# Top-k rounds ahead of the mixers' steps on VectorE, in the feed-forward stages of a two-layer trunk

## The chip, the cores and the metric

One core of a Trainium2 chip runs the whole kernel. The metric is the device time of one execution in microseconds (us). TensorE's clock has two levels, 1.2 and 2.4 GHz; the profile gives the granted clock as a share of full speed.

## The reference, cut to what matters

Two layers over a sequence of 1024 tokens, width 1024, float32. Each layer has three mixers side by side and then a feed-forward network:

```python
for l in range(DEPTH):                       # DEPTH = 2
    proj = rmsnorm(x, norm_mix[l]) @ w_in[l]
    y_a = s5_mixer(u, ...)                   # state space model, 16 groups
    y_b = dsa_attention(dq, dk, dv, iq, ik, iw, rel_bias)
    y_c = retention(rq, rk, rv, rg, ret_gn[l])
    x = x + concat(y_a, y_b, y_c) @ w_out[l]
    gate, up = split(rmsnorm(x, norm_ffn[l]) @ w_ffn_in[l], 2)
    x = x + (silu(gate) * up) @ w_ffn_out[l]     # D_FF = 2816
return rmsnorm(x, norm_final)
```

In `dsa_attention` an indexer scores every earlier position for each query, `lax.top_k` keeps 256 of them, and eight heads attend to these alone. The queries go in 8 blocks of 128; block b can see 128(b+1) keys, so blocks 0 and 1 need no choice.

## The kernel before, in words

The tokens are worked in two halves of 512. For layer l and half h there are three products: `proj` (18 units), `mixout` (8) and `ffn` (75). A **unit** is one 128-column slice of a weight matrix against all 512 tokens. Each number is split in a high and a low part, so a unit of `proj`, `mixout`, `gate` or `up` is 24 matmuls of 512 columns; a `down` unit is 12 (first of the four chunks of D_FF) or 18. Units write two psum banks in turn (A, B): unit i can begin only when unit i-2 has been read out. TensorE is the engine that should never stand.

Reading a unit out is VectorE's first work when the next unit has begun (the plan calls `ffn(..., i, ...)`, which handles unit i-1): the product of a gate with the row's scale (L1308), after which ScalarE applies Silu and GpSimd scales again; `up` times that (L1319); or the addition to x for a `down` unit (L1179). ScalarE also makes the high part of each weight tile (L835) and GpSimd the low part (L724).

All other work is cut into **steps** that stand in the plan behind a unit. Every engine walks the same list `PLAN` in order and issues its own part of each entry, so the order in the list is the order within each engine's queue. Three kinds matter here:

- `("round", b, r)`: one round of the top-k of block b, on VectorE alone (`top_round`): MAX8 finds eight largest scores of each row (L1359), MATCH_REPLACE8 strikes them out (L1361). Block b takes up to 32 rounds. Behind the last one a compare turns the scores into a mask (L1366 or L1368), which GpSimd needs for the attention of that block.
- `("attend", l, h, b, j, s)`: attention of block b for head pair j. In s=0 TensorE multiplies the probabilities of the pair before with the values and then makes the new logits (banks C and D). In s=1 VectorE adds mask and bias to the logits and takes the row's minimum of the negative (L1395, `nmax`, once for each head), ScalarE takes the exponential with that as bias (L1054), and TensorE transposes the result (L2079). These three stand in one step: TensorE reaches the transposes when the unit's matmuls are issued, and then needs VectorE's and ScalarE's part of the same step. With j=0, s=0 VectorE also makes the row sums of the block before (L1373, L1374), in s=1 it scales that block's output (L1381).
- `("scores", ...)` and `("retention", ...)`: the indexer's scores of a block (L1345 to L1352) and the pieces of the retention mixer (L1422 to L1483). In several of them too TensorE waits, at the end of the unit, for VectorE's part of the same step.

`weave(main, side)` (L84) deals the steps of a list over the units by estimated cost. It sorts what falls behind one unit; the sort is stable. The sides with both kinds are long in three stages: `ffn` of (0,0) and of (1,0), which carry the mixers of half 1 with the rounds of blocks 4 to 7, and `ffn` of (0,1), which carries those of layer 1, half 0, with the rounds of block 3. Other stages place their steps by hand or have no unit with both kinds behind it in another order.

In the stages of (0,0) and (1,0) the 96 rounds of blocks 5, 6 and 7 lie beside the attention of blocks 4, 5 and 6, which is 12 head pairs (four for each block). These stretches run from about 560 to 840 us and from 1851 to 2131 us; `ffn` of (0,1) with its mixers runs from 1111 to 1499 us.

Of the kernel before, what the change touches and what calls it, by code (L numbers as in the profile page):

```python
# [68 lines left out]
def cost(step):  # L69

    if step[0] == "round":
        return 2.2 * (NK[step[1]] + 150) / 1000
    return {"dma": 1.0, "diag": 1.0, "s5_prep": 3.0, "scores": 7.0}.get(step[0], 5.0)


def length(unit):

    kind, i = unit[0], unit[3]
    if kind == "ffn" and i < len(FFN) and FFN[i][0] == "down":
        return 3 * FF_CHUNKS[FFN[i][1]]  # L80
    return 3 * KT


def weave(main, side, first=0, last=None, rounds_last=True):  # L84


    last = len(main) if last is None else last
    total = sum(cost(s) for s in side) or 1.0
    time = sum(length(u) for u in main[first:last])
    out, n, spent, gone = [], 0, 0.0, 0  # L90
    for i, unit in enumerate(main):
        out.append(unit)
        gone += length(unit) if first <= i < last else 0
        share, behind = total * gone / time, []
        while n < len(side) and spent + cost(side[n]) / 2 <= share:
            spent += cost(side[n])
            behind.append(side[n])
            n += 1
        out += sorted(behind, key=lambda step: step[0] == "round") if rounds_last else behind
    return out + side[n:]  # L100


# [47 lines left out]
def plan():  # L150
# [16 lines left out]
    main = window("proj", 0, 0)  # L167
    side = [("boot", t) for t in range(TT + 1, NB + 2)] + [("bias", s) for s in range(3)]
    out += weave(main[:4], blend(param_steps(0), side)) + main[4:5] + [("rstd", "boot"), ("diag",)]
    sc = score_steps(0, 0)  # L170
    setup = [("s5_set", 0, s) for s in range(5)]
# [34 lines left out]
    def mix_and_ffn(l, h, side, lead):  # L206

        mix = window("mixout", l, h)
        ffn = window("ffn", l, h)
        got = []  # L210
        for n, unit in enumerate(mix[:N_OUT]):
            got += [unit] + (lead[n] if n < len(lead) else [])
        got += [("fillraw", DEPTH + l, 0)] + mix[N_OUT:] + [("fillraw", DEPTH + l, 1), ("sums", "inside")]
        got += ffn[:1] + scales() + weave(ffn[1:], side, 0, len(ffn) - 11)
        if (l, h) == (0, 0):

            for n, step in enumerate(param_steps(1)[:10]):
                got.insert(got.index(ffn[45 + 2 * n]), step)
        return got
# [4 lines left out]
    out += main[:1] + [("sums", None)]  # L224
    side = [("rstd", None), ("diag",), ("spread", "fill")] + [("dma", "load_xa", n) for n in range(4)] + param_steps(1)[10:14]
    out += weave(main[1:N_OUT], side)
    drain = main[N_OUT:]
    main = window("proj", 1, 0)
# [2022 lines left out]
```

## Time and profile before

| what | us |
|---|---|
| runs shown (3): median, lowest to highest | 2672.77, 2666.86 to 2673.14 |
| profiled execution: its own time | 2670.3 |
| its span, first to last instruction | 2668.5 |
| TensorE matmuls busy | 2551.4 (96%) |
| VectorE busy | 1553.0 (58%) |
| ScalarE busy | 1020.3 (38%) |
| GpSimd busy | 1308.9 (49%) |

Busy shares are means over stages: a slice of the 40 in the page's second part is 66.7 us, and there an engine at 58% over the span may be full for long stretches. A row of the timeline gives start, duration, engine, line, operation, output and inputs, and in brackets how long the engine stood before it and for whom. A matmul's duration (0.39 us for 512 columns) overlaps the next one's: from start to start it is 0.23 us.

### The profile page before, as it was taken

The page shows a single profiled execution, that of the slowest core. Times are in us where ns is not written, and L with a number is a line of the kernel's source. Part 1 is how long each engine was busy: PE and PEld are TensorE (multiplying, and loading weights), DVE is VectorE, ACT ScalarE, POOL GpSimd, SP SyncE. Part 2 cuts the span into 40 slices and gives each one's busy share as a digit, 9 for nine tenths or more (in the row PEclk, how much of TensorE's full clock was granted, in tenths as well). Part 3 has the DMA queues.
Part 4 walks back from the last instruction along what each step waited for, and adds up shares of the span by engine and source line. Part 5 has one row for each costly group of instructions (what it writes and reads, how often), then busy time and mean ns, then how long its engine had stood idle before and what let it go on. Part 6 is the DMA issues. An engine that isn't in the chain of part 4 may idle for free.

```text
span 2668.5 us, 34623 instructions
## 1 busy us (share of the span) xinstructions
PE 2551.4 (96%) x13515; PEld 2007.8 (75%) x13515; DVE 1553.0 (58%) x2691; ACT 1020.3 (38%) x1478; POOL 1308.9 (49%) x818
## 2 busy tenths in 40 slices
PE   8998979999999999999999999999999999999998
PEld 6766757677777777778777787777777777888887
DVE  3769767799997226833331385677999922211111
ACT  5232354244435433324344422442534453322222
POOL 3332344455545564536555532544555447665654
PEclk9988999999999999999999999999999999999998
DMA  5341112132222153323322242222222215233332
GB/s 165 85 132 41 49 53 90 52 91 72 78 71 64 58 189 95 87 64 91 91 77 82 80 138 56 79 60 76 77 77 60 79 44 201 79 103 103 108 110 82
DMA packets 385666, 232.91 MB, mean 87 GB/s; under 512 B 29593, under 2 KB 371553, under 8 KB 383073
## 3 DMA queue, kind: packets, MB, share of 16 engines
q1 hardware_dynamic: 385136, 229.62, 29.0%
q8 instruction: 109, 1.79, 0.3%
q10 hardware_dynamic: 368, 1.08, 0.1%
q14 instruction: 53, 0.43, 0.0%
HBM read 213.88 MB, written 14.69 MB: 86 GB/s over the span
## 4 chain that ended last, share of the span: by engine, by line
PE 68%; DVE 25%; ACT 3%; issue 3%; POOL 1%; DMA 1%; DVEq 0%; ACTq 0%; SPq 0%
PE psum L1759 65%; DVE scores L1361 7%; DVE top L1359 7%; PE psum L2079 1%; DVE psum L1395 1%; DVE xs L1179 1%; DVE scores L1347 1%; DVE tmp L1319 1%; ACT w_hi L835 0%; ACT scratch L1036 0%; POOL w_lo L724 0%; DVE tmp L1308 0%; DVE scratch L1428 0%; PE psum L2176 0%; ACT xs L1054 0%
## 5 line engine op out<-in xcount | busy, mean ns | idle before, releaser
L724 POOL TENSOR_TENSOR w_lo<-w_raw,w_hi 128x1024 fp32r<-128x1024 f32 (+2 forms) x408 | 900.8, 2208 | 1197.9 <-ACT w_hi L835 1197.8
L1759 PE MATMUL psum<-h_hi,w_hi 128*128 128x512 f32 x1984 | 796.4, 401 | 15.2 <-ACT h_hi L859 7.4
L835 ACT ACTIVATE w_hi<-w_raw 128x1024 fp32r<-128x1024 f32 (+2 forms) x408 | 397.7, 975 | 1047.9 <-PE psum L1759 989.4
L1759 PE MATMUL psum<-h_lo,w_hi 128*128 128x512 f32 x1984 | 763.2, 391 | 0.9 <-POOL h_lo L732 0.9
L1759 PE MATMUL psum<-h_hi,w_lo 128*128 128x512 f32 x1984 | 514.4, 390 | 0.0
L1759 PEld LDWEIGHTS psum<-h_hi,w_hi 128*128 128x128 f32 x1984 | 374.9, 189 | 128.3 <-issue 36.1
L1759 PEld LDWEIGHTS psum<-h_lo,w_hi 128*128 128x128 f32 x1984 | 373.9, 189 | 78.3 <-issue 1.9
L1759 PEld LDWEIGHTS psum<-h_hi,w_lo 128*128 128x128 f32 x1984 | 373.3, 188 | 76.6
L1359 DVE MAX8 top<-scores 128x8 f32<-128x512 f32 (+5 forms) x352 | 324.3, 921 | 7.8
L1361 DVE MATCH_REPLACE8 scores<-top,scores 128x512 f32<-128x512 f32 (+5 forms) x352 | 319.0, 906 | 0.0
L1179 DVE TENSOR_TENSOR xs<-xs,psum 128x512 f32<-128x512 f32 x160 | 109.6, 686 | 315.0 <-PE psum L1759 304.5
L1759 PE MATMUL psum<-a_hi,w_hi 128*128 128x512 f32 x704 | 279.2, 397 | 7.2 <-POOL a_lo L806 7.2
L1759 PE MATMUL psum<-a_lo,w_hi 128*128 128x512 f32 x704 | 274.9, 390 | 0.0
L1319 DVE TENSOR_TENSOR tmp<-psum,tmp 128x512 f32<-128x512 f32 x88 | 60.8, 691 | 245.0 <-PE psum L1759 243.9
L1759 PE MATMUL psum<-a_hi,w_lo 128*128 128x512 f32 x704 | 182.7, 393 | 0.0
L1759 PEld LDWEIGHTS psum<-a_hi,w_hi 128*128 128x128 f32 x704 | 132.6, 188 | 41.9 <-POOL a_lo L806 8.9
L1759 PEld LDWEIGHTS psum<-a_hi,w_lo 128*128 128x128 f32 x704 | 133.5, 190 | 28.1
L1759 PEld LDWEIGHTS psum<-a_lo,w_hi 128*128 128x128 f32 x704 | 132.7, 188 | 26.5
L806 POOL TENSOR_TENSOR a_lo<-tmp,a_hi 128x512 fp32r<-128x512 f32 x88 | 116.9, 1329 | 30.8 <-ACT a_hi L942 30.8
L1308 DVE TENSOR_TENSOR tmp<-psum,tmp 128x512 f32<-128x512 f32 x66 | 45.6, 691 | 122.1 <-PE psum L1759 114.8
L1759 PE MATMUL psum<-w_hi,h_hi 128*128 128x512 f32 x256 | 102.8, 402 | 4.4 <-ACT iqT L905 4.3
L1759 PE MATMUL psum<-w_hi,h_lo 128*128 128x512 f32 x256 | 100.5, 393 | 0.0
(310 smaller groups left out, 2913.5 us busy)
## 6 DMA issues: line engine op xcount, KB each, us to landing
w_raw<-in_w_ffn_in_dram SPq DMA_DIRECT2D x176, 512.0 KB, 3.8
w_raw<-in_w_ffn_out_dram SPq DMA_DIRECT2D x96, 384.0 KB, 3.1
w_raw<-in_w_in_dram SPq DMA_DIRECT2D x68, 512.0 KB, 3.8
w_raw<-in_w_out_dram SPq DMA_DIRECT2D x32, 512.0 KB, 3.6
x_half<-xs SPq DMA_DIRECT2D x8, 1024.0 KB, 6.5
xs<-x_half SPq DMA_DIRECT2D x8, 1024.0 KB, 6.9
w_raw<-in_w_ffn_out_dram SPq DMA_DIRECT2D x32, 256.0 KB, 2.7
out_dram<-mixed SPq DMA_DIRECT2D x8, 512.0 KB, 4.5
```

What stands on the lines that cost most here:

```text
L724: eng.tensor_tensor(w_lo(u, n), w_raw[:, u % 3, 0:n], w_hi[:, u % 2, 0:n].bitcast(F32), ALU.subtract).then_inc(sems["weights_ready"], 1)
L806: eng.tensor_tensor(a_lo[:, f, :], atmp, a_hi[:, f, :].bitcast(F32), ALU.subtract).then_inc(sems["a_lo_ready"], 1)
L835: act(w_hi[:, u % 2, 0:n], w_raw[:, u % 3, 0:n], ACTF.Copy).then_inc(sems["hi_ready"], 1)
L1179: tt(xs[:, m, :], xs[:, m, :], bank(g), ADD).then_inc(sems["x_added"], 1)
L1308: tt(scaled, bank(g), row, MUL).then_inc(sems["gated"], 1)
L1319: tt(atmp, bank(g), gate, MUL).then_inc(sems["atmp_ready"], 1)
L1347: ins = stt(score[b], bank(g, 0, NK[b]), w, score[b], MUL, ADD)
L1359: eng.max(out=top8[:, :], in_=src).then_inc(sems["round_step"], 1)
L1361: eng.match_replace(out=src, in_to_replace=top8[:, :], in_values=src, imm_value=TAKEN).then_inc(sems["round_step"], 1)
L1395: eng.tensor_tensor_reduce(bank(g, 0, nk), bank(g, 0, nk), at_.mask(b, n), -1.0, 3e38, ADD, ALU.min, nmax[:, i:i + 1]).then_inc(sems["nmax ...
L1759: return eng.matmul(out_, lhsT, rhs, start=start, stop=stop, skip_group_check=True)
L2079: ins = eng.transpose(bank(g, k * P, (k + 1) * P), at_.prob[:, n, k * P:(k + 1) * P], ident)
```

## The change

```diff
-def weave(main, side, first=0, last=None, rounds_last=True):
+def weave(main, side, first=0, last=None, sort_rounds=True):
...
-        out += sorted(behind, key=lambda step: step[0] == "round") if rounds_last else behind
+        out += sorted(behind, key=lambda step: step[0] != "round") if sort_rounds else behind
```

Before, the steps behind a unit stood with the mixers' steps first and the rounds last. Now the rounds stand first and the mixers' steps behind them. No step moves to another unit, and none is added or dropped; the order among rounds, and among the others, stays. No call passes the last parameter. The order changes behind 85 units: 36 of `ffn` (0,0), 36 of `ffn` (1,0) and 13 of `ffn` (0,1). Rounds issue on VectorE alone, so only VectorE's queue has another order; the queues of TensorE, ScalarE, GpSimd and SyncE stand as before, the DMAs too.

## Rows read from the trace of the kernel before

**Rows 1.** The page's slices: busy tenths of TensorE and VectorE over the span.
```profile
PE   8998979999999999999999999999999999999998
DVE  3769767799997226833331385677999922211111
```

**Rows 2.** The page's chain of work that ended last, by line.
```profile
PE psum L1759 65%; DVE scores L1361 7%; DVE top L1359 7%; PE psum L2079 1%; DVE psum L1395 1%; DVE xs L1179 1%; DVE scores L1347 1%; DVE tmp L1319 1%; ACT w_hi L835 0%; ACT scratch L1036 0%; POOL w_lo L724 0%; DVE tmp L1308 0%; DVE scratch L1428 0%; PE psum L2176 0%; ACT xs L1054 0%
```

**Rows 3.** Windows: PE, PEld, DVE, ACT, POOL busy us, PEclk, DMA share, GB/s.
```profile
560.00:840.00 280.00, 269.88 (x1453) 214.26 (x1453) 269.81 (x393) 122.39 (x163) 148.28 (x100) 0.99 0.26 75
1111.00:1499.00 388.00, 385.46 (x1927) 304.05 (x1925) 135.14 (x254) 155.73 (x247) 198.81 (x134) 1.00 0.28 81
```

**Rows 4.** Groups of VectorE by form, 560 to 850 us: busy us, mean ns.
```profile
L1359 DVE MAX8 top<-scores 128x8 f32<-128x1024 f32 x32 | 39.2, 1224 | 0.6
...
L1359 DVE MAX8 top<-scores 128x8 f32<-128x896 f32 x32 | 34.9, 1091 | 0.7
...
L1359 DVE MAX8 top<-scores 128x8 f32<-128x768 f32 x32 | 30.7, 958 | 0.7
L1361 DVE MATCH_REPLACE8 scores<-top,scores 128x768 f32<-128x768 f32 x32 | 30.2, 943 | 0.0
```

**Rows 5.** Timeline of the unit that began at 575.80, attention (4, pair 0).
```profile
575.80 0.39 PE L1759 MATMUL psum<-h_hi,w_hi 128*128 128x512 f32 x1
...
577.84 0.69 DVE L1308 TENSOR_TENSOR tmp<-psum,tmp 128x512 f32<-128x512 f32 x1
...
578.44 0.82 DVE L1395 CUSTOM_DVE_ANT_0 psum<-psum,scores 128x640 f32<-128x640 f32 x1
...
579.21 1.28 ACT L1054 ACT_TABLE_LOAD   x1
...
579.42 1.98 PE L1759 MATMUL psum<-h_hi,w_lo 128*128 128x512 f32 x8
...
580.50 0.80 ACT L1054 ACTIVATE scratch<-psum,nmax 128x640 f32<-128x640 f32 x1
...
581.53 1.51 PE L2079 MATMUL psum<-cst,scratch 128*128 128x128 f32 x10
...
582.80 0.47 PE L1759 MATMUL psum<-h_hi,w_hi 128*128 128x512 f32 x1
```

**Rows 6.** Timeline of the unit that began at 681.15, attention (5, pair 1).
```profile
681.15 0.39 PE L1759 MATMUL psum<-h_hi,w_hi 128*128 128x512 f32 x1
...
683.87 0.96 DVE L1395 CUSTOM_DVE_ANT_0 psum<-psum,scores 128x768 f32<-128x768 f32 x1
...
684.92 0.90 ACT L1054 ACTIVATE scratch<-psum,nmax 128x768 f32<-128x768 f32 x1 [0.30 <-DVE nmax L1395]
...
686.60 1.47 PE L2079 MATMUL psum<-cst,scratch 128*128 128x128 f32 x12
```

**Rows 7.** Timeline, attention (6, pair 1): late read-out, Silu, late values.
```profile
764.64 0.69 DVE L1308 TENSOR_TENSOR tmp<-psum,tmp 128x512 f32<-128x512 f32 x1
...
767.71 1.75 PE L1759 MATMUL psum<-scratch,vw 128*64 128x128 f32 x28 [2.51 <-ACT scratch L1036]
```

**Rows 8.** TensorE's waits before transposes, timeline; and one window as in rows 3.
```profile
807.52 2.84 PE L2079 MATMUL psum<-cst,scratch 128*128 128x128 f32 x14 [2.27 <-ACT scratch L1054]
...
892.42 3.12 PE L2079 MATMUL psum<-cst,scratch 128*128 128x128 f32 x16 [2.71 <-ACT scratch L1054]
...
807.90:811.40 3.50, 3.50 (x16) 3.17 (x15) 3.43 (x4) 1.47 (x3) 2.84 (x3) 0.51 0.25 48
```

**Rows 9.** Timeline of scores and retention, four waits between 459 and 551 us.
```profile
459.03 2.34 DVE L1347 SCALAR_TENSOR_TENSOR scores<-psum,vw,scores 128x896 f32<-128x896 f32 x2 [2.94 <-ACT psum L1029]
...
485.38 1.97 PE L2106 MATMUL psum<-cst,scratch 128*128 128x128 f32 x16 [1.50 <-DVE scratch L1428]
...
544.85 1.22 DVE L1469 TENSOR_REDUCE gsum<-scratch 128x16 f32<-128x1024 f32 x1 [1.67 <-ACT scratch L1082]
...
550.18 0.47 PE L1759 MATMUL psum<-h_hi,w_hi 128*128 128x512 f32 x1 [1.41 <-DVE xs L1179]
```

## The prediction

> **What bounds the kernel now.** I read the page's slices first: TensorE stands at 9 tenths nearly everywhere, VectorE at 7 to 9 in two places, slices 9 to 13 and again 28 to 32 [rows 1]. The chain says the same: 65% of it is TensorE's unit matmuls, but 14% is rounds (L1359 and L1361) and 1% is L1395 [rows 2]. So in those two places VectorE's queue sets the end. The windows size it: from 560 to 840 us TensorE is busy 269.9 of 280 and VectorE 269.8 of 280; in the third stage that the change touches VectorE is busy 135 of 388 and TensorE 385 [rows 3]. The first two are balanced to a hair: neither engine has slack, so what counts is who waits for whom, and a new wait of TensorE on VectorE costs nearly its length. The third has slack on VectorE. Last I read the timeline unit by unit, noting when TensorE began a unit, when VectorE read out the one before, and what ended TensorE's wait at its end.
>
> **What an attention step looks like.** The unit that begins at 575.80 has its last matmuls until 581.40. VectorE comes 2.0 late, reads out at 577.84 and goes straight to nmax at 578.44; ScalarE's exponential follows at 580.50 and the transposes begin at 581.53, just as the matmuls end. The next unit starts at 582.80 [rows 5]. The rounds of that unit run beside the transposes and the next unit. nmax is thus the one piece of VectorE's work with a near deadline, and it stands first. The step of (5, pair 1) is alike: nmax 683.87, exponential 684.92, transposes 686.60, which the matmuls and not the exponential delayed [rows 6].
>
> **The change, priced.** Nothing is added or removed; VectorE's busy time stays. The rounds of a unit now stand ahead of nmax. A round is MAX8 and MATCH_REPLACE8 and about 0.14 us between: 0.958 + 0.943 gives 2.05 us for block 5, and from MAX8's 1.091 and 1.224, with a replace of like length, 2.3 us for block 6 and 2.55 us for block 7 [rows 4].
>
> The way from the start of nmax to the first transpose is 1.05 us to the exponential, 0.90 of it and 0.2 for its sum: 2.15 us at 768 columns [rows 6], so about 1.85 at 640 and 2.4 at 896. The table load at 579.21 began before the first nmax had ended [rows 5]; with rounds in between it is hidden, so it isn't in these sums.
>
> First place, (4, pair 0): nmax would start 2.65 us into the unit; with two rounds (4.1) it is 6.75, and the transposes come at 8.6 where the matmuls end at 5.6. TensorE stands 3.0. The next unit starts at 9.9 where it was 7.0: +2.9. Is it given back? VectorE leaves nmax early against the next unit (about 1 us before it starts, its read-out done), runs that unit's two rounds in 4.1 and then must wait for the unit to end at 5.7. It idles 2.5, which it did not before. Two units on it is as late (0.9) as it was. So the delay stays, since VectorE was full before.
>
> I carried this from place to place in one long stage (the other has the same 36 changes and the same windows). For each: rounds ahead, start of the transposes after the unit's first matmul, growth of the time to the next unit.
> - (4,0): 2 rounds, 8.6, +2.9. (4,1): 2 rounds, 7.55, +2.4. (4,2): 3 rounds, 9.55, +4.4. (4,3): 1 round behind a `down` unit (4.1 us of matmuls), 4.85, +0.6.
> - (5,0): 1, 5.95, +0.9. (5,1): 2, 8.95, +3.8. (5,2): 1, 6.65; here VectorE was 3.4 late before and is 1.5 late now: -0.5. (5,3): 2, 7.65, +2.5.
> - (6,0): 2, 6.2, +0.9. (6,1): 1, 6.5, +2.6. (6,2): none. (6,3): 2, 8.5, +3.3.
>
> Sum of the growing ones 24.3 us. Against it stands what VectorE's idling buys. Before, it was so late at some units that the read-out itself held ScalarE: at 764.64 it read out a gate that had ended 3.7 earlier, Silu and the copies of the transposed probabilities came behind, and TensorE stood 2.51 us before the values [rows 7]. Being less late there gives 2.2 back, likewise 1.2 before (6, pair 0) and 1.2 at (6, pair 2), where it stood 2.27 [rows 8]. With the 0.5 that is 5.1. Net 19.2 per stage.
>
> **Scores and retention, at the head of the stage.** Here the new order also helps. Before the scores VectorE stood 2.94 us for ScalarE [rows 9]: a round of block 4 (about 1.7) now fits in. The same holds for the second score step, and TensorE's next unit comes 1.5 earlier. Then retention's rotation, for which TensorE already waited 1.50 us at 485.38, gets two rounds ahead; VectorE is 2 us less late by then, and of the 1.5 about 0.7 survives. At 544.85 VectorE stood 1.67 for ScalarE [rows 9]; a round fits there as well, and the wait of 1.41 for a read-out at 550.18 goes. But two units on, two rounds and one more stand ahead of the last retention products and take 1.5 back. Net -0.6 per stage, between -3 (no loss) and +3 (the rotation loses its two rounds in full).
>
> The third stage: only steps with a deadline matter, and VectorE idles there. The rotation of retention gets a round of block 3 ahead, +1.4, since TensorE waits for it already by my reading of the timeline. Attention steps there start nmax at the unit's start, so a round of 1.5 stays under 5.6 of matmuls. Zero for these; if that cover were gone it would be up to 1.5 at each of three.
>
> **The clock.** After the wait of 2.27 us TensorE's clock fell to its lower level: 0.51 of full speed from 807.90 to 811.40, and likewise after the 2.71 at 892.42 [rows 8]; the wait of 2.51 at 767.71 brought none. A fall of 3.4 us at half speed loses at most 1.7 us; I take 1.5, since ScalarE paces part of it. In the new kernel the waits of TensorE are 3.0, 1.95, 3.95, 3.35, 2.05, 2.25 and 2.9 us at the seven large places. I count four falls a stage (the three longest and one of the rest) less half a fall saved at (6, pair 2): 4 x 1.5 - 0.75 = 5.2. Bounds are 0 and 7 x 1.7 = 12.
> The Trainium skill, "TensorE: Matmul & The Clock Gate" (What's actually happening), says the throttled state is the default and activity releases it. Its table of recommendations warns against idle gaps between bursts of matmuls, which speaks against this change. The trace agrees for two waits and not for 2.51. If each of the seven waits brought a fall, it would be the third rival below.
>
> **Sum.** 2 x (19.2 - 0.6) + 1.4 + 2 x 5.2 = 49 us on the profiled execution's own 2670.3 (span 2668.5): 2719. The median of the runs shown, 2672.8, lies 2.5 above that execution and the lowest 3.4 below it, so it needs no shift.
>
> **Rivals.**
> - *VectorE's total decides.* In the long stages VectorE is 96% busy and its work is unchanged; a stall of TensorE could be absorbed, as VectorE catches up while TensorE stands. For it: the -5.1 above is exactly that. Against it: to absorb, VectorE must have work to catch up on, and at most places it is only 1 to 2 us late and then runs into the unit's end. If all but the 10 us by which VectorE's windows are not full were absorbed, about +8: 2678.
> - *The rounds fill VectorE's waits* (the other side). VectorE now has rounds to do while ScalarE or TensorE finish what its next step needs. Rows 9 show 2.94, 1.67 us of such waits. If only these counted, because nmax keeps slack under the unit's matmuls, it would be 2 x (1.5 + 1.4) = 6 less: 2664. It decides where rounds ahead of nmax stay shorter than the slack; rows 5 show that slack as 0.1 us where the rounds are 4.1, so this can be true only if VectorE is far ahead of TensorE, and it isn't.
> - *The clock falls after every long wait.* 2 x (7 x 1.5 - 0.75) in place of 2 x 5.2: +9, 2728.
> - *The delay spreads.* ScalarE's queue stands at the exponential until nmax comes, and behind it are the high part of the next weights (L835), Silu and the copies; GpSimd's low parts follow. I took these as hidden, as a weight tile is made a unit ahead. If each of the seven large waits lost another 2 us by this (a table load and a copy), it is +28: 2747.
>
> **How the numbers follow.** Forecast 0.60, VectorE's total 0.12, filling 0.04, clock 0.12, spreading 0.12. The measurement tells about 0.3%, 8 us, from nothing. Faster by more than that only with the filling: 0.04. Within: most of VectorE's total: 0.08. Slower: 0.88. The forecast's own range is 2700 to 2738 (the clock's bounds and half of the bounds of the head of the stage); for 8 in 10 I take 2690 to 2744.
>
> **What would show it.** In the profile after: VectorE's and TensorE's busy us unchanged; both long windows about 25 us longer, with VectorE near 91% there. A wait of "PE L2079 <- ACT L1054" in the list of waits that grows from under 5 us to about 20 per stage, and ScalarE's wait for nmax with it. The clock below 1.0 in several stretches of the long stages. TensorE's wait before the values of (6, pair 1) gone. The third stage the same within 3 us. It is wrong if TensorE's transposes still begin right behind the matmuls, or if VectorE stays at 96%.

## The result, and the profile after

| | before | after |
|---|---|---|
| median (lowest to highest), us, 4 runs each | 2671.78 (2666.86 to 2673.14) | 2726.41 (2725.55 to 2730.22) |
| profiled execution: own time, span | 2670.3, 2668.5 | 2725.6, 2723.5 |
| granted clock, mean over the span | 0.987 | 0.978 |

The kernel is slower: ratio 1.021, 95% interval 1.0198 to 1.0222, or +54.6 us. The forecast was 2719 (range 2690 to 2744), +49 on the profiled execution's own time where it was +55.

The page's slices after, which answer to [rows 1]: where VectorE stood at 9 in its two long stretches (slices 9 to 12 and 29 to 32), it now stands mostly at 8 in the first and at 7 to 9 in the second.
```profile
PE   8998989989999999999999999998999989999998
DVE  4769767788898225833331395677789932211112
```
The chain after, which answers to [rows 2]. TensorE's units have 70% where they had 65, the rounds 11% where they had 14; TensorE's transposes have 2% where they had 1, and ScalarE's exponential is new with 1%.
```profile
PE psum L1759 70%; DVE scores L1361 6%; DVE top L1359 5%; PE psum L2079 2%; DVE xs L1179 1%; ACT scratch L1054 1%; DVE tmp L1319 1%; POOL w_lo L724 1%; ACT w_hi L835 0%; ACT scratch L1036 0%; ACT xs L1054 0%; PE psum L1904 0%; DVE psum L1395 0%; PE psum L2106 0%; DVE scores L1347 0%
```
Windows, columns as in [rows 3], cut at the same units before and after: from the start of the unit of (4, pair 0) to the start of the one after (6, pair 3), in the first long stage and in the second. The first two rows are before, the last two after.
```profile
575.80:837.55 261.75, 252.70 (x1373) 200.90 (x1372) 253.56 (x369) 114.74 (x155) 134.91 (x91) 0.99 0.26 75
1867.31:2128.55 261.24, 251.39 (x1373) 199.47 (x1372) 253.56 (x369) 114.65 (x155) 134.96 (x91) 1.00 0.25 73
...
579.21:865.31 286.10, 261.65 (x1373) 206.21 (x1372) 256.41 (x373) 113.57 (x154) 134.91 (x90) 0.96 0.24 70
1897.32:2185.79 288.47, 264.02 (x1373) 208.34 (x1372) 256.82 (x373) 114.52 (x155) 135.66 (x91) 0.95 0.23 68
```
The two stretches are 24.4 and 27.2 us longer. TensorE is busy 9.0 and 12.6 us more with the same 1373 matmuls, at a granted clock of 0.96 and 0.95 where it was 0.99 and 1.00, and it stands 15.4 and 14.6 us more. VectorE is busy 90% and 89% of them; it was 97%.

The group of VectorE by form, as in [rows 4]: MAX8 at 768 columns takes the same 958 ns, and VectorE is busy 1551.4 us over the whole run where it was 1553.0. No work was added to it.
```profile
L1359 DVE MAX8 top<-scores 128x8 f32<-128x768 f32 x32 | 30.6, 958 | 0.7
```
The timeline of attention (4, pair 0), which answers to [rows 5]. The unit starts at 579.21. VectorE reads out at 581.25, as late as before, but nmax comes at 585.95, 6.74 us into the unit, behind two rounds. The exponential waits 2.97 for it, and the transposes begin 8.7 us into the unit, having stood 3.09. The table load is over long before.
```profile
579.21 0.39 PE L1759 MATMUL psum<-h_hi,w_hi 128*128 128x512 f32 x1
...
581.25 0.69 DVE L1308 TENSOR_TENSOR tmp<-psum,tmp 128x512 f32<-128x512 f32 x1
...
582.62 1.28 ACT L1054 ACT_TABLE_LOAD   x1
...
585.95 0.83 DVE L1395 CUSTOM_DVE_ANT_0 psum<-psum,scores 128x640 f32<-128x640 f32 x1
...
586.87 0.79 ACT L1054 ACTIVATE scratch<-psum,nmax 128x640 f32<-128x640 f32 x1 [2.97 <-DVE nmax L1395]
...
587.90 1.52 PE L2079 MATMUL psum<-cst,scratch 128*128 128x128 f32 x10 [3.09 <-ACT scratch L1054]
...
589.18 0.52 PE L1759 MATMUL psum<-h_hi,w_hi 128*128 128x512 f32 x1
```
The same of (4, pair 2), the largest place with three rounds, and of (5, pair 1), which answers to [rows 6]. The waits are 3.97 and 3.27 us. At 647.86, one unit on from (4, pair 2), VectorE's read-out waits 5.37 us for TensorE. In the stretch of the windows above VectorE now stands over 1 us at six places, and it stood so at none before. It has nothing to catch up with.
```profile
636.30 0.83 DVE L1395 CUSTOM_DVE_ANT_0 psum<-psum,scores 128x640 f32<-128x640 f32 x1
...
638.26 2.37 PE L2079 MATMUL psum<-cst,scratch 128*128 128x128 f32 x10 [3.97 <-ACT scratch L1054]
...
647.86 0.69 DVE L1308 TENSOR_TENSOR tmp<-psum,tmp 128x512 f32<-128x512 f32 x1 [5.37 <-PE psum L1759]
...
707.46 0.97 DVE L1395 CUSTOM_DVE_ANT_0 psum<-psum,scores 128x768 f32<-128x768 f32 x1
...
709.65 2.79 PE L2079 MATMUL psum<-cst,scratch 128*128 128x128 f32 x12 [3.27 <-ACT scratch L1054]
```
What is given back, against [rows 7]: the values of (6, pair 1) wait 0.46 us where they waited 2.51.
```profile
791.91 1.75 PE L1759 MATMUL psum<-scratch,vw 128*64 128x128 f32 x28 [0.46 <-issue]
```
The clock, against the window of [rows 8]: two windows after, at the waits of 3.09 and 3.97 us. The last column but two reads 0.50, that is 1.2 GHz, for 3.4 and for 6.8 us. The third row is a fall at the stage's head, at the wait of 3.96 shown next. The last row is the wait before the transposes of (4, pair 1), and the clock is at 0.50 from 613.4 to 616.8 there too.
```profile
589.50:592.90 3.40, 3.40 (x9) 2.63 (x8) 2.57 (x4) 1.70 (x3) 3.33 (x2) 0.50 0.00 0
637.30:644.10 6.80, 5.84 (x19) 5.10 (x20) 5.09 (x9) 4.06 (x8) 4.47 (x4) 0.50 0.00 0
562.20:569.00 6.80, 6.01 (x18) 5.07 (x19) 4.48 (x6) 2.21 (x3) 6.38 (x6) 0.50 0.01 2
...
612.04 1.59 PE L2079 MATMUL psum<-cst,scratch 128*128 128x128 f32 x10 [1.93 <-ACT scratch L1054]
```
The head of the stage, which answers to [rows 9]. The four waits were 2.94, 1.50, 1.67 and 1.41: the first is 1.35, the second 1.67, the third 0.36 and the fourth gone, the unit starting at 547.2, 3.0 earlier than before. The last row is new: TensorE stands 3.96 us for the last retention product.
```profile
458.84 2.34 DVE L1347 SCALAR_TENSOR_TENSOR scores<-psum,vw,scores 128x896 f32<-128x896 f32 x2 [1.35 <-ACT psum L1029]
...
483.82 1.97 PE L2106 MATMUL psum<-cst,scratch 128*128 128x128 f32 x16 [1.67 <-DVE scratch L1428]
...
543.64 1.22 DVE L1469 TENSOR_REDUCE gsum<-scratch 128x16 f32<-128x1024 f32 x1 [0.36 <-ACT scratch L1082]
...
562.99 1.97 PE L2160 MATMUL psum<-cst,scratch 128*128 128x128 f32 x8 [3.96 <-DVE scratch L1483]
```
Last the waits of the whole run, in us, times, longest. ScalarE's for nmax was 42.2 in 22 waits before. TensorE's before the transposes is the second row before and the third after: 36 us more.
```profile
ACT scratch L1054 <- DVE nmax L1395: 103.8, 36, 6.2
PE psum L2079 <- ACT scratch L1054: 14.8, 8, 2.7
PE psum L2079 <- ACT scratch L1054: 50.7, 24, 4.0
```

### The profile page after: what moved, and what is told of

Read it like the earlier page. It is cut to its first block, busy times and chain, and to the rows that moved or that the text cites. A ratio compares the mean times of both kernels' runs of the same rounds, so it can differ in the third digit from the quotient of the medians.

```text
span 2723.5 us, 34616 instructions
## 1 busy us (share of the span) xinstructions
PE 2577.5 (95%) x13515; PEld 2025.8 (74%) x13515; DVE 1551.4 (57%) x2691; ACT 1019.5 (37%) x1478; POOL 1311.3 (48%) x818
## 3 DMA queue, kind: packets, MB, share of 16 engines
q10 hardware_dynamic: 368, 1.08, 0.1%
## 4 chain that ended last, share of the span: by engine, by line
PE 74%; DVE 19%; ACT 3%; issue 3%; POOL 1%; DMA 1%; DVEq 0%; ACTq 0%; SPq 0%
PE psum L1759 70%; DVE scores L1361 6%; DVE top L1359 5%; PE psum L2079 2%; DVE xs L1179 1%; ACT scratch L1054 1%; DVE tmp L1319 1%; POOL w_lo L724 1%; ACT w_hi L835 0%; ACT scratch L1036 0%; ACT xs L1054 0%; PE psum L1904 0%; DVE psum L1395 0%; PE psum L2106 0%; DVE scores L1347 0%
## 5 line engine op out<-in xcount | busy, mean ns | idle before, releaser
L1759 PE MATMUL psum<-h_hi,w_hi 128*128 128x512 f32 x1984 | 807.6, 407 | 10.7 <-ACT h_hi L859 6.7
L1759 PE MATMUL psum<-h_lo,w_hi 128*128 128x512 f32 x1984 | 772.4, 396 | 0.9 <-POOL h_lo L732 0.9
L1759 PEld LDWEIGHTS psum<-h_hi,w_hi 128*128 128x128 f32 x1984 | 382.4, 193 | 125.8 <-issue 31.3
L1759 PEld LDWEIGHTS psum<-h_lo,w_hi 128*128 128x128 f32 x1984 | 380.1, 192 | 80.3 <-issue 1.9
L2079 PE MATMUL psum<-cst,scratch 128*128 128x128 f32 x496 | 76.7, 305 | 51.8 <-ACT scratch L1054 50.7
L1054 ACT ACTIVATE scratch<-psum,nmax 128x640 f32<-128x640 f32 (+7 forms) x96 | 77.7, 812 | 104.1 <-DVE nmax L1395 103.8
```

Source lines behind the costliest of these rows:

```text
L1054: act(at_.prob[:, n, 0:nk], bank(g, 0, nk), ACTF.Exp, scale=-1.0, bias=nmax[:, i:i + 1], accum_out=rsum[:, i:i + 1]).then_inc(sems["p_read ...
L1759: return eng.matmul(out_, lhsT, rhs, start=start, stop=stop, skip_group_check=True)
L2079: ins = eng.transpose(bank(g, k * P, (k + 1) * P), at_.prob[:, n, k * P:(k + 1) * P], ident)
```

## Experiments

Except for the filler, each replaces the line of the changed `weave` that sorts the steps behind a unit. A step is a tuple: for "attend" its last three fields are block, pair and half; half 1 holds nmax, exponential and transposes, and half 0 of pair 0 also finishes the row sums of the block before. The experiments were run in three sets, each with its own runs of the kernel before, whose medians were 2672.2, 2669.1 and 2673.0 us. A ratio is always to the kernel before of the same set; where medians of different sets are compared, they are uncertain by some 4 us.

**Is it the rounds ahead of nmax?** Two kernels that are complements: the first takes before's order behind units with half 1 and the new order elsewhere, the second the reverse.
```
+ near = any(step[0] == "attend" and step[5] for step in behind)
+ out += sorted(behind, key=lambda step: (step[0] == "round") == near)
```


> The changed kernel, but behind a unit with an attention step s=1 (nmax) the mixers' steps stand first again, as before the change; behind all other units the rounds stay first. Theory (the cost is nmax standing behind rounds with TensorE's transposes waiting for it): the 18 or so growing places go; what is left is the head of the stages (-1.5, -1.4, +0.5, +3.8 and a clock fall of +2.1 each in the trace after), so 2672 + 7 = 2679 us, at most 2685, and the granted clock returns to about 0.985. Rival (any mixer step behind rounds costs, nmax is only one of them): about half of the 54 us stays, 2700. Rival (VectorE's total decides): no difference, 2726.

Measured: 2689.8 against 2672.2, ratio 1.0071 (1.0057 to 1.0085). Most of the loss is gone, but 2679 to 2685 was expected.
```
+ out += sorted(behind, key=lambda step: (step[0] == "round") != near)
```


> The kernel before, but behind a unit with an attention step s=1 (nmax) the rounds stand first; all other units have the order of before. The complement of e1. Theory: nearly the whole cost comes from here, 2718 to 2724 us, and the two parts add up to the change (e1 + e2 - before = 2726 within 4 us). If the order behind the other units matters by itself: 2700 or less.

Measured: 2725.1, ratio 1.0200 (1.0181 to 1.0220). The order at nmax alone makes nearly the whole loss, 52.8 of 54.6 us. But the rest isn't free either: +17.5 us by itself, and 52.8 + 17.5 = 70 is more than the 54.6 of both together. So the two interact.

**Where does the first kernel lose?** Set side by side unit by unit, it loses most behind the units with row sums: 4.8 and 5.9 us in one long stage, 4.2 and 3.4 in the other. Its timeline at the second of them: RECIPROCAL and COPY stand behind two rounds, and TensorE waits 3.29 us for their result. The COPY took 0.43 us at this place before and takes 1.67 here, having begun inside an instruction of GpSimd (more on that below).
```profile
756.81 0.20 DVE L1374 RECIPROCAL rinv<-rsum 128x8 f32<-128x8 f32 x1
...
757.04 1.67 DVE L1375 COPY scratch<-rinv 128x512 f32<-128x512 f32 x1
...
758.77 2.08 PE L1760 MATMUL psum<-cst,scratch 128*128 128x128 f32 x8 [3.29 <-DVE scratch L1375]
```
I then kept before's order at each step I took for one with a deadline:
```
+ near = any(step[0] == "attend" and (step[5] or step[4] == 0) or step[0] == "retention" and step[3] in (2, 13)
+            for step in behind)
+ out += sorted(behind, key=lambda step: (step[0] == "round") == near)
```


> Rounds stand first only behind units whose mixers' steps have no near deadline; they stand last behind units with nmax, with the row sums (attention s=0 of pair 0), with retention's rotation (step 2) or its last product (step 13). Theory: the gains of the scores (1.5 us) and of the read-out at the end of the first chunk (1.4 us) remain in each of the two long stages and nothing is paid: 2672 - 6 = 2666 us, between 2662 and 2670. Rival (what is gained early is lost in the balanced stretch, where VectorE is the bound): 2672, no change.

Measured: 2679.3, ratio 1.0028 (1.0017 to 1.0039). A miss, by 13 us. Of it 5.0 and 6.3 us (one per long stage) arise behind one unit with retention's step 4, which had not been on my list. Its rows (line numbers two above those of before): L1442 is still of step 3; it takes 3.42 us where it took 1.75 before, having begun inside an instruction of GpSimd. VectorE is late by it, step 4 (L1449) comes behind two rounds, and TensorE, done with its unit's matmuls at 496.64, starts the next unit at 505.50. A fall of the clock at 501.9 is in it too. In the changed kernel the same unit has its rounds ahead as well and did not grow at all; L1440 took 1.22 us there. So rounds ahead of step 4 cost nothing by themselves.
```profile
491.61 3.42 DVE L1442 TENSOR_TENSOR scratch<-mixed,cst 128x1024 f32<-128x1024 f32 x1
...
499.11 0.76 DVE L1449 TENSOR_TENSOR scratch<-psum,cst 128x256 f32<-128x256 f32 x2
```

**Do the row sums cost in the changed kernel too?** First with only the row sums ahead of the rounds and all else as changed, then with nmax and row sums both ahead:
```
+ near = any(step[0] == "attend" and step[4:] == (0, 0) for step in behind)
```


> The changed kernel, with the mixers' steps first again behind the 8 units that carry the row sums (attention s=0 of pair 0). In e1 these units grew by 5 to 6 us each, where VectorE came late to them. Theory (what a step pays for rounds ahead depends on how late VectorE is; in the changed kernel TensorE's waits for nmax have made it early): no difference, 2724 to 2728. Rival (rounds ahead of the row sums cost 4 to 6 us at each place whatever stands before): about 2710.

Measured: 2723.7, ratio 1.0205 (1.0174 to 1.0235); 2.7 below the changed kernel, whose ratio of 1.021 lies in this interval. That is what the theory said.
```
+ near = any(step[0] == "attend" and (step[5] or step[4] == 0) for step in behind)
```


> As e1 (nmax first, other rounds first; 2690), with the row sums first too. Left with rounds first are scores, retention and nothing of attention with a deadline. Theory: e1's growth at the row sums (4.8 and 5.9 us in the first stage, 4.2 and 3.4 in the second, and some 1 us at the last blocks) goes: 2672 + 2 x 3.4 from the head of the stages = 2679, at most 2683. Rival (e1's surplus is spread over the stage, a lateness that goes on): 2688 to 2690.

Measured: 2674.4, ratio 1.0020 (1.0008 to 1.0031), 15.3 below the first experiment, or 14 by the two ratios. So the same edit is worth some 14 us where nmax stands first and nothing that can be told where the rounds stand ahead of it. There TensorE's new waits have let VectorE catch up, and a round ahead of the row sums is then done in time: in the traces of the first experiment TensorE stands 2.5, 3.3 and 1.0 us for the row sums of blocks 4 to 6, in those of the changed kernel not over 0.3 us for any. That is the interaction.

**Does the cost follow the number of rounds?** Only the first round goes ahead of an nmax step; all else as before.
```
+ near = any(step[0] == "attend" and step[5] for step in behind)
+ ahead = [step for step in behind if step[0] == "round"][:1] if near else []
+ out += ahead + sorted([s for s in behind if s not in ahead], key=lambda step: step[0] == "round")
```


> The kernel before, with one round, not all, ahead of nmax behind each unit of an attention step s=1. A smaller dose of e2 (which measured 2725). If a round costs only beyond the slack (nmax's start in the unit, plus the round, plus 1.85 to 2.4 us to the transposes, against the unit's 5.6 or 4.2): +0.9 at (4,0), 0.6 at (4,3), 2.2 at (5,0), 1.7 at (5,1), 1.3 at (5,2), 2.6 at (6,1), 0.3 at (6,3), 0 elsewhere, less 2 to 3 given back: 2672 + 2 x 8 = 2688. No clock falls, since no wait passes 3 us. If cost were in proportion to the rounds moved (11 of 19 in a stage): 2703.

Measured: 2686.7, ratio 1.0064 (1.0042 to 1.0086). The sum held, +14.5 for a forecast of about 16, place by place in the first long stage: 0.9 at (4, pair 0) for 0.9, 0 at pairs 1 and 2, 2.6 for 2.6 at (6, pair 1), -2.5 at (6, pair 2). Off by over 1 us were (4, pair 3), 1.8 for 0.6, and (5, pair 2), -0.5 for +1.3. Moving 11 of the 19 rounds costs 14.5 us and moving all costs 52.8: the first round hides under what slack there is. The clock's part of the expectation failed. Its trace has falls at 667.3 and 2073.6, at waits of 1.84 and 2.20 us, where none was expected below 3 us.

**What do the clock's falls cost?** In the changed kernel, matmuls into a free bank, whose results nobody reads, stand in TensorE's queue ahead of the transposes at six places with long waits. The order of VectorE's steps is the changed one.
```
+ fill = {(4, 1): 8, (4, 2): 16, (5, 1): 13, (5, 3): 8, (6, 1): 8, (6, 3): 11}.get((b, j), 0)
+ if fill:
+     take("F")
+     for _ in range(fill):
+         mm(bank("F"), h_hi[:, 0, 0:P], h_hi[:, 0, :], True, True)
```


> The changed kernel with matmuls that nobody reads (512 columns, 0.23 us each) in front of the transposes at six places a long stage, 8 to 16 of them, as many as fit in TensorE's wait for the exponential. They take no time that TensorE had not stood. Theory (the falls of the granted clock are a cost of their own, about 1.6 us behind each long wait): the falls at these six places go, in the trace 1.6 + 1.7 + 0.5 + 0.8 in the first stage and as much or more in the second, so 8 to 10 us less than the changed kernel, 2717. Rival (the clock costs nothing beyond the wait): 2726 to 2729, same or a little slower.

Measured: 2713.4 (2710.6 to 2716.7), ratio 1.0162 (1.0146 to 1.0177), 13.0 below the changed kernel, where 8 to 10 were expected. Its timeline at (4, pair 2): TensorE is busy 3.33 us where it had stood, and 0.34 us of wait are left.
```profile
632.18 3.33 PE L1759 MATMUL psum<-h_hi 128*128 128x512 f32 x14
...
635.85 1.52 PE L2084 MATMUL psum<-cst,scratch 128*128 128x128 f32 x10 [0.34 <-ACT scratch L1054]
```
Its window of the long stage: the granted clock is 0.99 where it was 0.96.
```profile
560.00:870.00 310.00, 295.88 (x1576) 233.01 (x1576) 277.33 (x404) 127.00 (x170) 156.85 (x107) 0.99 0.25 70
```
The time at the lower level, 2 x (1 - clock) x span, is 2 x 0.022 x 2723.5 = 120 us after and 76 us here; it was 69 before. The falls at these places, less what the filler itself delays, are 13 of the 54.6 us. By the starts of units the two stretches of attention are 6.7 and 9.5 us shorter with it. The waits themselves are the larger part: TensorE stands 30 us more in these two stretches of the changed kernel, by the windows above.

**Are there places where rounds ahead pay?** The forecast's head of the stage said so of the scores and of retention's step 10. These alone:
```
+ free = any(step[0] == "scores" or step[0] == "retention" and step[3] == 10 for step in behind)
+ out += sorted(behind, key=lambda step: (step[0] == "round") != free)
```


> The kernel before, with rounds first only behind the units of the last score steps and of retention's step 10 (4 units in each long stage), where VectorE stood for ScalarE: the trace after shows 1.5 us gained at the second score step and 1.4 at the read-out behind step 10, and nothing paid there. Theory: 3 us in each long stage and kept to the end, since what follows is TensorE's order as before: 2666 us, against 2672 before. Rival (VectorE's total is the bound in the balanced stretch, so an earlier start is all that helps and only part stays): 2669 to 2672, no change that can be measured.

Measured: 2672.0 against 2669.1, ratio 1.0010 (0.9997 to 1.0023). A miss: the scores gained as expected, the retention step lost it again. Its timeline (line numbers one above those of before): two instructions of VectorE that read SBUF twice take 2.71 and 3.31 us, each begun inside one of GpSimd's that makes a low part. Before, the same two took 1.47 and 1.23.
```profile
544.89 2.49 POOL L725 TENSOR_TENSOR w_lo<-w_raw,w_hi 128x1024 fp32r<-128x1024 f32 x1 [2.10 <-ACT w_hi L836]
...
545.76 2.71 DVE L1474 TENSOR_TENSOR scratch<-scratch 128x1024 f32<-128x1024 f32 x1
...
552.99 2.65 POOL L725 TENSOR_TENSOR w_lo<-w_raw,w_hi 128x1024 fp32r<-128x1024 f32 x1 [1.59 <-ACT w_hi L836]
...
553.43 3.31 DVE L1481 TENSOR_TENSOR scratch<-scratch,gn_row 128x1024 f32<-128x1024 f32 x1
...
562.22 1.36 PE L2161 MATMUL psum<-cst,scratch 128*128 128x128 f32 x8 [4.09 <-DVE scratch L1484]
```
To test the cause, the kernel above without GpSimd's subtraction for three units per long stage; ScalarE copies the raw weight there, so the low part of these units is another number and the output with it:
```
+ if u % 204 in (61, 62, 63):                      # gpsimd: no low part of these
+     return
...
+ if u % 204 in (61, 62, 63):                      # scalar: a copy instead
+     eng.wait_ge(sems["weights_ready"], u)
+     act(w_lo(u, n), w_raw[:, u % 3, 0:n], ACTF.Copy).then_inc(sems["weights_ready"], 1)
```


> e5 (rounds first behind score steps and retention's step 10), and the low parts of the weights of three units in each long stage (those around retention's steps 10 to 13) are written by ScalarE as a plain copy of the raw weights, not by GpSimd as the difference; the product is another, the work of TensorE and VectorE the same. Theory (L1473 and L1480 were stretched by GpSimd's instruction): both take 1.2 us again, VectorE's chain is 3.5 us shorter, TensorE's wait at the end of the unit before retention's last product falls from 5 to about 1.5 and the clock's fall behind it goes: 8 to 9 us less than e5, 2663. Rival (VectorE has that much work there anyway): both keep 2.7 and 3.3, time as e5.

Measured: 2664.7, ratio 0.9972 (0.9961 to 0.9984). That is 7.3 below the kernel it is built on by the medians of two sets, and 10 by the two ratios, whose intervals lie apart. Both instructions are back at 1.22 us, TensorE's wait is 2.26 and its product starts at 558.26 instead of 562.22; 1.2 of these 4.0 us it was ahead before the place already. By the starts of units the place is 2.8 us shorter in the first long stage and 5.6 in the second, where a fall of 6.8 us goes with it (line numbers six above those of before):
```profile
544.52 1.22 DVE L1479 TENSOR_TENSOR scratch<-scratch 128x1024 f32<-128x1024 f32 x1
...
551.56 1.22 DVE L1486 TENSOR_TENSOR scratch<-scratch,gn_row 128x1024 f32<-128x1024 f32 x1
...
558.26 1.97 PE L2166 MATMUL psum<-cst,scratch 128*128 128x128 f32 x8 [2.26 <-DVE scratch L1489]
```
So with the retention step left out, the scores alone should pay, and they need no such trick:
```
+ free = any(step[0] == "scores" for step in behind)
+ out += sorted(behind, key=lambda step: (step[0] == "round") != free)
```


> The kernel before, with rounds first only behind the three units of the last score steps in each long stage. In e5 the trace is 2.5 us ahead of before until retention's step 10, and the 1.5 won there is lost with more on the next three units, where VectorE's retention instructions with both operands in SBUF (L1473, L1480) took 2.7 and 3.3 us in place of 1.2, while GpSimd's subtraction for the weights ran. Theory (these instructions wait for GpSimd's when they start inside one; with scores alone the retention steps keep their place against the units and GpSimd): 2.5 us kept in each long stage, 2667 against 2672. Rival (VectorE's total in the balanced stretch takes any early gain back): same as before.

Measured: 2661.6 (2658.2 to 2664.9) against 2673.0, ratio 0.9961 (0.9946 to 0.9975). This version beats both kernels; it lies 11 us below the one before. Its timeline of the place [rows 9] begin with (line numbers one above): VectorE's wait of 2.94 is 1.35. The units behind the score steps start 3.0 and 3.2 us earlier in the two long stages, 1.6 us of it at the second score step and 1.6 behind retention's rotation, to which VectorE comes less late. All of it is kept in the first stage and 2.7 us in the second. So about 6 us are explained, for 5 expected. The rest goes with clock falls of before that are missing (9 stretches at the lower level in place of 12, 55 us in place of 71), and those come and go between kernels for reasons I haven't shown.
```profile
459.25 2.34 DVE L1348 SCALAR_TENSOR_TENSOR scores<-psum,vw,scores 128x896 f32<-128x896 f32 x2 [1.35 <-ACT psum L1030]
```
On top of it, the filler at the two places where before's clock fell [rows 8], (6, pair 2) with 8 matmuls and (7, pair 3) with 11:
```
+ fill = {(6, 2): 8, (7, 3): 11}.get((b, j), 0)
```


> e9, and matmuls that nobody reads in two waits that the kernel before has already: 8 before the transposes of (6, pair 2), 11 before those of (7, pair 3). Theory (the clock falls behind these waits at 807.9, 893.3 and 2183.5 in the trace before cost some 1.4 us each): 3 to 4 us less than e9, 2663. Rival (falls of the clock move elsewhere or cost nothing): as e9.

Measured: 2665.7 (2658.3 to 2668.7), ratio 0.9971 (0.9958 to 0.9984). No gain. Behind (7, pair 3) the starts of units come 1.4 us earlier in both long stages, as expected. But falls stand at other places now (911.7, 993.7, 1003.9), and the first of them takes 1.6 us back. In these kernels filler paid 13 us over twelve waits of about 2 to 4 us, and nothing over four of 2.2 to 2.7.

## Why the prediction was right, and where it was off

Shifts of TensorE's unit starts between the two traces, against the forecast's terms:

| term | forecast, us | measured, us |
|---|---|---|
| attention, first long stage, growing places | +24.3 | +24.9 |
| the same, given back | -5.1 | -7.2 |
| clock behind its waits | +5.2 | +5.7 |
| attention, second long stage, all | +24.4 | +27.2 |
| head of the long stage | -0.6, -0.6 | +3.6, +3.0 |
| third stage | +1.4 | about -1.2 |
| the remainder | 0 | -1.0 |
| sum | +49 | +55 |

- *The place is the bound and a wait of TensorE costs nearly its length*: right. The growth by place, forecast then measured, was 2.9 and 2.96, 2.4 and 2.35, 4.4 and 5.13, 0.6 and 0.59 in block 4; 0.9 and 0.26, 3.8 and 4.64, -0.5 and -0.55, 2.5 and 3.11 in block 5; 0.9 and 0, 2.6 and 2.56, 0 and -2.48, 3.3 and 3.32 in block 6. The -2.48 is the term that I had in the part given back. (The table's first three measured terms make 23.4 and the shift over the stage's attention is 24.4. The difference is in the remainder: most of it is 0.84 us lost behind the unit at 839.8, one unit after 0.63 of the part given back was won.) The remainder has more in it, most of all falls of the clock that stand at other places in the two executions: +1.6 between the stages, with falls at 1023.0 and 1033.2 after, and -1.4 and -2.2 later in the run, where before had more of them (one at 1500.9, and 16 us at the lower level behind 2620 for 10 behind 2678 after).
- *VectorE has nothing to catch up on*: right. The rival in which its total decides gave 2678 and rested on 96% in the windows of [rows 3]; cut at the same units it was 97% and is 90% now (I had said near 91), and the read-out one unit after (4, pair 2) waits 5.37 us. Only the picture of two busy places was too simple: VectorE stands at 6 to 9 tenths in slices 2 to 8 of [rows 1] too, which the change doesn't touch.
- *The clock*: five falls came in the first stretch where I counted four, but the term was too small, and that the sum of a stretch came out is luck. Falls behind the waits of the first long stage cost 1.58, 1.60, 1.76 and 0.77 us in the next units, 5.7 for 5.2. But the transposes after the waits ran at the lower level as well (2.79 us at 709.65 for 1.47 in [rows 6], 2.37 at 638.26), and that lies in the growth by place above. By the windows cut at the same units TensorE stands 15.4 us more in the first stretch, where the waits less the part given back were put at 19.2, and is busy 9.0 us more, where the clock was put at 5.2: 24.4 for 24.4, since the two errors cancel. In the second it is 14.6 and 12.6. The forecast's sign that TensorE's busy time stays was wrong for the same reason: 2551.4 us before, 2577.5 after. The filler experiment gives 13 us for the whole run. The wait of 1.93 us at (4, pair 1) brought a fall as well, where [rows 7] show 2.51 without, so the length of a wait alone doesn't tell.
- *The head of the stage* is the mis-sized term: -0.6 was forecast, +3.6 and +3.0 came. The gains came as forecast: -1.54 behind the scores, -1.43 at the read-out. I had the last retention product cost 1.5; behind it the shift grew by 0.54 and 3.78, and by 2.08 more with the clock's fall of 6.8 us at 562.2. I had counted rounds only, and neither the stretch of VectorE's instructions beside GpSimd's (2.71 for 1.47 in the changed kernel too, at 546.97) nor a fall. The bound that I gave, +3, was just too low. Which share the stretch has in the changed kernel itself wasn't run; in the two kernels that differ by GpSimd's instructions the place was 2.8 and 5.6 us shorter without them, falls of the clock included.
- *The third stage*: I had a round ahead of the rotation at +1.4; the rotation cost 0.3, and the unit before it gained 1.5. A miss of 2.6 us. The same 1.5 stands in the traces of the kernels that keep the new order behind that unit and in none of those that don't, so it belongs to the round there; why it is won wasn't taken apart.
- *The rounds fill VectorE's waits*, the rival on the other side: its mechanism is real where no deadline of TensorE follows, and only there. Kept at the scores alone it is worth 11 us by the medians, of which about 6 were traced to these steps.
- *The delay spreads*: no place lost 2 us beyond its wait. The largest excess is at (5, pair 1), 4.64 for 3.8, and its transposes at the lower clock level are 1.3 us longer than in [rows 6].
- *The range*: the forecast's own bounds (0 and 12 us of clock a stage, half of the bounds of the head) give 2706 to 2736, not 2700 to 2738. The range for 8 in 10 was wider and held.

## What to carry to other kernels

Where two engines are balanced, order one engine's queue by who waits for each step: what another engine needs within the unit goes first, filler work behind it, and where the engine waits for others itself, filler goes ahead. List every step that TensorE awaits before trusting such a rule; the row sums and retention's step 4 were missing from mine, and each cost 3 to 6 us where VectorE was late. Look too at what a moved step will run beside: an instruction with both inputs in SBUF that slides under one of GpSimd can lose 2 us. What an order costs depends on how late the engine already is, so the prices of two edits don't add.

## What the runs showed of the hardware

VectorE's TENSOR_TENSOR with both inputs in SBUF, 128x1024, takes 1.22 us alone. It takes 2.71 or 3.31 in the rows above, where it starts inside a GpSimd TENSOR_TENSOR of 2.49 or 2.65 us. It ended 1.1 us after GpSimd's in both (548.47 for 547.38, 556.74 for 555.64), as if it had begun its work only then. With GpSimd's instruction gone it was 1.22 both times. The traces of all thirteen kernels here say the same. They hold 676 such instructions of VectorE. The 350 that didn't begin inside a TENSOR_TENSOR of GpSimd took 1.21 to 1.23 us, also where GpSimd's began while they ran; of the 326 that did, 325 ended 1.08 to 1.11 us after GpSimd's end, the other having begun 1 ns after GpSimd's start. So the time of such an instruction is told by where GpSimd's ends and not by its own work. MAX8, MATCH_REPLACE8 and the read-outs with a PSUM operand kept their times (MAX8 at 768 columns 958 ns on average over 32, before and after). The COPY of the row sums in the first experiment did not: 1.67 us for 0.43. The Trainium skill, "SBUF — State Buffer" (SBUF: two separate sides), tells of a port pair that the two engines share and that whichever starts first holds for its whole instruction, while the other waits; for a VectorE instruction with two SBUF inputs it says so against a GpSimd instruction that reads SBUF. The trace agrees.
